# First attention of a fused two-block layer: the imaginary S5 input products of tiles 8 to 15 read a copy of the branch input whose partition halves are exchanged, in other row groups of TensorE

## The reference, cut to what matters

```python
    uf = u.astype(f32).reshape(B, S, S5_GROUPS, S5_GROUP_CH)
    ...
    bu_r = jnp.einsum('bsgh,gph->bsgp', uf, bbar_r)
    bu_i = jnp.einsum('bsgh,gph->bsgp', uf, bbar_i)
    ...
    _, _, xr, xi = lax.associative_scan(_complex_affine_combine, (a_r, a_i, bu_r, bu_i), axis=1)
    y = (jnp.einsum('bsgp,ghp->bsgh', xr, c_re.astype(f32))
         - jnp.einsum('bsgp,ghp->bsgh', xi, c_im.astype(f32)))
```

## Time and profile before

| | value |
|---|---|
| runs | 1992.41, 1983.17, 1986.96 us |
| median | 1986.96 us |
| span of the profiled execution | 1982.0 us |
| PE busy | 1873.8 us (95%) |
| DVE, ACT, POOL busy | 959.8, 523.0, 332.9 us |
| mean granted clock of PE | 0.987 |
| bytes moved | 396.88 MB |

### The profile page before, as it was taken

One profiled execution on the slowest core, in us unless ns is written; L12 is line 12 of the kernel. 1 busy time (PEld: TensorE's weight loads), 2 busy tenths in 40 slices (PEclk: granted clock), 3 DMA queues, 4 the chain that ended last, 5 costly groups with the idle time before them and its releaser, 6 DMA issues. The chain is left out here.

```text
span 1982.0 us, 27981 instructions
## 1 busy us (share of the span) xinstructions
PE 1873.8 (95%) x10606; PEld 1040.9 (53%) x10606; DVE 959.8 (48%) x2029; ACT 523.0 (26%) x1154; POOL 332.9 (17%) x297
## 2 busy tenths in 40 slices
PE   8999999999998999999999998999988999999997
PEld 3434448845443344444444443457745588888443
DVE  4987748732375232332332335623375554444643
ACT  2448831101311233333333332220255100000000
POOL 0655530000027110010010014300023000000000
PEclk9999999999999999999999999999999999999999
DMA  6129972204355999999999999613310122222311
GB/s 249 64 80 231 230 217 99 81 5 152 145 195 170 359 406 405 403 402 404 407 407 405 400 402 372 239 68 118 128 43 1 43 105 87 85 85 85 129 62 43
DMA packets 85535, 396.88 MB, mean 200 GB/s; under 512 B 13394, under 2 KB 13650, under 8 KB 60240
## 3 DMA queue, kind: packets, MB, share of 16 engines
q1 hardware_dynamic: 55728, 303.59, 40.1%
q10 hardware_dynamic: 16880, 58.52, 10.2%
q0 software_dynamic: 12848, 33.74, 4.7%
HBM read 374.66 MB, written 55.09 MB: 217 GB/s over the span
## 5 line engine op out<-in xcount | busy, mean ns | idle before, releaser
L2823 DVE COPY slab<-bank 32x512 f32<-32x512 f32 x124 | 80.8, 688 | 400.2 <-PE bank L1476 400.2
L1089 PE MATMUL bank<-ring,slab 128*128 128x512 f32 (+1 forms) x608 | 254.6, 578 | 6.5 <-DVE slab L2291 3.8
L1468 PE MATMUL bank<-slab 128*32 128x512 f32 x1536 | 228.9, 599 | 17.1 <-DMA ring<-w_exp_down 6.6
L1468 PE MATMUL bank<-ring,slab 128*32 128x512 f32 x1536 | 228.5, 598 | 14.6 <-DVE slab L2779 5.1
L1476 PE MATMUL bank<-ring,slab 128*32 128x512 f32 x512 | 228.5, 599 | 0.0
L1476 PE MATMUL bank<-slab 128*32 128x512 f32 x480 | 214.0, 599 | 0.0
L1089 PEld LDWEIGHTS bank<-ring,slab 128*128 128x128 f32 x608 | 115.7, 192 | 139.1 <-issue 130.4
L3225 POOL TENSOR_TENSOR small<-small 128x1 f32<-128x1 f32 (+2 forms) x30 | 27.5, 920 | 817.1 <-DVE small L2288 817.1
L1468 PEld LDWEIGHTS bank<-slab 128*32 128x32 f32 x1536 | 73.5, 110 | 145.7 <-issue 139.8
L1089 PE MATMUL bank<-slab,ring 128*128 128x512 f32 (+1 forms) x368 | 148.2, 559 | 1.7 <-ACT slab L1831 0.9
L1468 PEld LDWEIGHTS bank<-ring,slab 128*32 128x32 f32 x1536 | 72.3, 110 | 144.9 <-issue 142.2
(11 more groups left out here) (363 smaller groups left out, 3053.7 us busy)
## 6 DMA issues: line engine op xcount, KB each, us to landing
ring<-stream SPq DMA_DIRECT2D x173, 512.0 KB, 4.4
slab<-w_exp_gu SPq DMA_DIRECT2D x64, 1024.0 KB, 13.8
ring<-w_exp_gu SPq DMA_DIRECT2D x64, 1024.0 KB, 13.6
ring<-w_exp_down SPq DMA_DIRECT2D x32, 1024.0 KB, 22.3
slab<-w_exp_down SPq DMA_DIRECT2D x32, 1024.0 KB, 23.0
y_rows<-zeros ACTq DMA_DIRECT2D x1, 24960.0 KB, 132.0
y_rows<-slab ACTq DMA_DIRECT2D x64, 384.0 KB, 8.2
gb<-rows ACTq DMA_DIRECT2D x5, 512.0 KB, 4.4
```

Source lines behind the costliest of these rows:

```text
L1089: mm = nc.tensor.matmul(dst, lhs[k], rhs[k], start=(k == 0), stop=(k == len(lhs) - 1))
L1468: mm = nc.tensor.matmul(g_bank[32 * g:32 * g + 32, :], x[:, k, 32 * g:32 * g + 32], w[:, 512 * k:512 * k + 512], start=(k == 0), stop=(k = ...
L2823: i = nc.vector.tensor_copy(ye[b % 2][32:64, 512 * half:512 * half + 512], bank[5 + half][96:128, :])
```

## The change

The diff does five things. On the host, the imaginary input weights of tiles 8 to 15 are laid 64 partitions away from their place (modulo 128). In the ACT program, at the end of the exponentials of heads 0 and 1, two transfers from SBUF to SBUF each copy one 128 x 512 block of `uT` (blocks 2 and 3) with its lower and upper 64 partitions exchanged, into blocks 0 and 1 of slab3, where the keys of heads 0 and 1 lay; ahead of them is a wait for the fourth score tile of that head. `s5_in(i)` for `i` of 8 and above reads the copy for its imaginary product, at partitions `(r0 + 64) % 128`; at tiles 8 and 12 PE waits for the copy (`u_moved`, 32 = both halves). The imaginary states of tiles 8 and 11 move from slab3 block 0 to `s5tmp`, and that of tile 14 to slab3 block 2. POOL's wait for scores moves from tile 8 (`s` 3) to tile 14 (`s` 11).

```diff
--- before.py
+++ after.py
@@ -38,6 +38,7 @@
 XH, XD = 4, 128
 NG, NS, NCH = 32, 64, 16
 NST = NG * NS // P
+S5_TURNED = NST // 2
 NE, TOPK, NGRP, TOPG = 64, 8, 8, 4
 CAP = 96
 NOV = T * TOPK // CAP
@@ -533,7 +534,8 @@
             for g in range(2):
                 grp = 2 * i + g
                 r = 32 * (i % 4) + 16 * g
-                bm[n, r:r + 16, i // 4, 64 * g:64 * g + 64] = w[b][0, grp].T
+                rb = (r + 64) % P if n == 1 and i >= S5_TURNED else r
+                bm[n, rb:rb + 16, i // 4, 64 * g:64 * g + 64] = w[b][0, grp].T
                 cm[n, 64 * g:64 * g + 64, i, 16 * g:16 * g + 16] = w[c][0, grp].T
     return np.concatenate([bm[0].reshape(P, 512), bm[1].reshape(P, 512),
                            cm[0].reshape(P, 512), cm[1].reshape(P, 512)], 1)
@@ -614,7 +616,10 @@
         s5xr, s5xt = [unit(13), unit(14)], unit(17)
 
         def s5xi(i):
-            return unit(15 + i % 3) if i % 3 < 2 else s5tmp if i < 8 else fm(slab3, 0)
+            return unit(15 + i % 3) if i % 3 < 2 else s5tmp if i < 14 else fm(slab3, 2)
+
+        def u_turned(j):
+            return fm(slab3, j - 2)
 
         cmask = rope_q
         b_re = gb[:, 0:512].rearrange("p (j n) -> p j n", j=4)
@@ -879,6 +884,7 @@
         s5_tab, s5_z, s5_x, s5_used, s5_c = sem("s5_tab"), sem("s5_z"), sem("s5_x"), sem("s5_used"), sem("s5_c")
         rope_arg, rope_tab, krope_ready, khat_ready = sem("rope_arg"), sem("rope_tab"), sem("krope_ready"), sem("khat_ready")
         max_ready, probs_ready = sem("max_ready"), sem("probs_ready")
+        u_moved = [sem("u_moved0"), sem("u_moved1")]
         y_ready, gelu_ready = sem("y_ready"), sem("gelu_ready")
         merged_ready = sem("merged_ready")
         x2_stored, tab_zero = sem("x2_stored"), sem("tab_zero")
@@ -1103,9 +1109,17 @@
                 return [p[:, (at + k) * P:(at + k + 1) * P] for k in range(kn)]
 
             def s5_in(i):
-                r = slice(32 * (i % 4), 32 * (i % 4) + 32)
-                for name, m in (("s5r", b_re), ("s5i", b_im)):
-                    product(name, i, [m[r, i // 4, :]], [fm(uT, i // 4)[r, :]])
+                j, r0 = i // 4, 32 * (i % 4)
+                r = slice(r0, r0 + 32)
+                product("s5r", i, [b_re[r, j, :]], [fm(uT, j)[r, :]])
+                if i < S5_TURNED:
+                    product("s5i", i, [b_im[r, j, :]], [fm(uT, j)[r, :]])
+                else:
+                    if i % 4 == 0:
+                        pe.wait_ge(u_moved[j - 2], 32)
+                    r1 = (r0 + 64) % P
+                    ri = slice(r1, r1 + 32)
+                    product("s5i", i, [b_im[ri, j, :]], [u_turned(j)[ri, :]])
 
             def s5_out(i):
                 if i % 4 == 0:
@@ -1927,6 +1941,10 @@
                         x = probs(h, qt)
                         nc.scalar.activation(x, x, ACT.Exp, scale=-1.0, bias=nmax[:, qt:qt + 1],
                                              accum_out=rsum[:, qt:qt + 1]).then_inc(probs_ready, 1)
+                if h < 2:
+                    full("s", 4 * h + 3)
+                    for r in (0, 64):
+                        act.dma_start(u_turned(2 + h)[64 - r:128 - r, :], fm(uT, 2 + h)[r:r + 64, :]).then_inc(u_moved[h], 16)
                 if h >= 3 and h % 2 == 1:
                     o = (h - 3) // 2
                     copy("o", o, fm(oT, o), tile("o", o)[:, :])
@@ -3247,8 +3265,8 @@
                     pool.wait_ge(s5_x, i)
                 if i >= 2:
                     pool.wait_ge(s5_used, i - 1)
-                if i == 8:
-                    pool.wait_ge(psum_full, plan.full("s", 3))
+                if i == 14:
+                    pool.wait_ge(psum_full, plan.full("s", 11))
                 c, s = s5cos[i % 2], s5sin[i % 2]
                 zr, zi, xr, xi = s5zr[i % 2], s5zi[i % 2], s5xr[i % 2], s5xi(i)
                 op = nc.gpsimd.tensor_tensor
```

## The result

The changed kernel takes 2098.88 us (median of 4 runs, 2094.37 to 2103.09) against 1988.12 us before (4 runs). The ratio is 1.056, with a 95% interval of 1.0536 to 1.0585. The profiled execution of the changed kernel has a span of 2092.4 us and took 2094.37; before, the span was 1982.0. The difference of the spans is 110.4 us, that of the medians 110.8.

A forecast was written before the change was run, and what follows sets the result against it. PE was taken to bound the kernel, busy 1873.8 of 1982.0 us. Wait 114.3 + clock 2.9 - row groups 3.4 = +113.8 us, giving 2100.8 on the median 1986.96; predicted 2100, range 2082 to 2112.

The forecast's parts named there:

- the wait for the fill: The forecast case: at tile 8 PE waits 114.3 us for copies behind the fill, and pairs overlap; chance 0.72.
- The copy's place in the queue: On ACT's queue q10, taken to go in order, the copies land behind the fill of 24960 KB.
- When the fill lands: Fill takes 128 us, landing at 266.7; copy there at 268.0, so PE waits 114.3 us (98.5 to 118).
- The clock: After PE's wait the clock is granted at 0.50 for a while, costing 2.9 us (0 to 6).
- The other row groups: The two `s5_in` products of a tile overlap in different row groups, saving 0.86 us a pair (0 to 0.96).
- Which pairs count: Only tiles 9 to 12 of eight pairs save time, 3.4 us (0 to 6.7); from head 6 others set the pace.
- The rest: ACT's two issues, 0.45 us each, lie in its idle 3.55 us; POOL's wait, new state places and host weights cost nothing.
- rival B: ACT itself is held at the first copy's issue, freed shortly before the fill ends; at worst some 5 us added; chance 0.12.
- Two of the signs that I had named: In the profile after: second pair of copies landing at some 90 to 110 us; DVE, ACT and POOL empty from about 160.
- A: The copy passes the fill and lands in time; PE waits 0 to 3 us at tile 8, 1980 to 1987; chance 0.08.
- C: The halves of PE's array don't work at once; the 3.4 us saving is missing, 2104; chance 0.08.

The follow-up runs named there:

- run 1: Changed kernel with the fill of zeros issued by ACT behind the second pair of copies instead of ahead of the loop; 1983.95 us, ratio 0.9972.
- run 4: Changed kernel with the copies issued by SP on the weight panels' queue, the fill where it was; 1983.62 us, ratio 0.9974.
- run 5: Changed kernel, fill and copies on ACT as they are, but PE reads the original branch input in old row groups without waiting for copies; 2082.25 us, ratio 1.0458.
- Run 8: run 1 repeated (0.9980), with only tiles 8 to 12 in the other row group (0.9980), and with tiles 4 to 6 there too (0.9970).
- run 3: Kernel before the change with only the fill moved to head 1; 1989.50 us, ratio 1.0005.
- run 7: Changed kernel with a fifth of the fill ahead of the copies, four fifths behind the second pair; 2004.42 us, ratio 1.0067.
- run 2: Against run 1: copies made without the exchange, imaginary products of tiles 8 to 15 in the real ones' row group; 1993.35 us, ratio 1.0008 of before.

## Why the prediction was right, by its steps

I had forecast 2100 (2082 to 2112), slower, with the chance on the wait for the fill. The time was 2098.88. That it is within 1.1 us is partly luck: the sum was +113.8 us and the medians moved by 110.8, 3.0 less, but the median of before rose from 1986.96 to 1988.12 with a fourth run, and 0.8 us had been rounded off.

- **The copy's place in the queue.** Right, and shown by runs 1 and 4: the same copies take 2.3 us ahead of the fill, 9.8 on another queue during it, and 120.8 behind it. The order seen in the earlier trace rows, a 12 KB load that lands 13.0 us after its issue, pointed that way. It could not by itself tell order in a queue from mere traffic; run 4 does. (It was not the last to land either, as the prediction has it: a 32 KB load issued behind it, at 287.25, landed after 13.4 us, at 300.7.)
- **When the fill lands.** I took 128 us (the sum goes by 128.2); it ran in 125.7, and in 130.0 in run 5. PE's wait was 111.3 us and not 114.3, inside 98.5 to 118. The fill's own time explains 2.5 us of the difference; its earlier issue in this execution goes with an earlier tile 8 and nearly cancels.
- **The clock.** 2.9 us predicted from one gap of 4.8 us; measured 1.04 (imaginary product 2.00 instead of 0.96) + 2.53 (gate product) = 3.6. The length of the wait matters little: after waits of 13.6, 50.8 and 111.3 us the imaginary product takes 2.07 us each time and the gate product 9.32, 9.49 and 9.66.
- **The other row groups.** A pair takes 1.06 us instead of 1.91: 0.85 saved, 0.86 predicted from products of 64 rows. By the Trainium skill, "TensorE: Matmul & The Clock Gate", Part 3, as cited in the prediction, the pair would take 0.96, an estimate; the measurement decides, and stays 0.1 above.
- **Which pairs count.** Four were to count, 3.4 us; the trace gives 3.34. It adds up from the other end too: tiles 9 to 15 are seven pairs, 7 x 0.85 = 5.95, and PE's waits at the end of the attention grow by 0.8 (5.6 for 4.8), 0.9 (1.20 for 0.30) and 0.9 (a wait for ACT's gate copy that was not there before), 2.6 together. Run 8 shows it directly. With tile 8's pair whole, as in run 1, five count: 4.25 by this rule, 4.0 seen.
- **The rest.** Here I was wrong in a part that did not show in the sum. I wrote that the two issues on ACT, 0.45 us each, lie in its idle time. The first took 94.19 us. It was rival B (chance 0.12) that described this, and in place B was right: ACT was held, and freed 26 us before the fill ended. But B and the forecast do not exclude each other; B's price of up to 5 us on top was near 0, since ACT was back at work 26 us before PE was. Two of the signs that I had named failed with it: the second pair of copies, which I had put at about 160, was issued at 246.14 and landed after 18.2 us, not 90 to 110; and ACT, empty before that, was at work again from 237.87. Neither cost time, since tile 12 needs the second pair much later. Run 5 shows what B alone costs: 91 us. My reason against it, that the fill's own issue took only 0.64 us, says nothing of the one behind it.

Rivals A and C are out: no copy passed the fill on its queue, and the pairs do overlap.

**The better version.** The row groups are worth having once the copies do not stand behind the fill: 0.9972 (0.9954 to 0.9990) with the fill behind them, 0.9974 (0.9957 to 0.9991) with the copies on SP's queue, both against before. The repeat of the first gave 0.9980 (0.9960 to 1.0000). That is 3 to 6 us by the medians and 3.7 to 4.0 by the stretch from tile 8 to head 9, held against run 3, 0.2 to 0.3% of the time; the interval of the repeat reaches 1.

## What to carry to other kernels

Before a small transfer is put on a queue, look for the largest one that is still under way there, and count the bytes ahead, not the bytes of the transfer: here a copy of 128 KB took 121 us because 25.6 MB stood in front. A DMA issue is not free for its engine either: behind a large transfer the issue itself may hold the engine and all that it does for others, even when nobody waits for the data. A large transfer that nobody waits for belongs behind every small one that somebody does, or on a queue of its own; and a saving on the busiest engine counts only in stretches in which that engine does not wait for the others.

## What the runs showed of the hardware that was not expected

**An issue that holds its engine.** ACT's next issue behind the fill of 4 KB pieces was let go when some 26 to 28 us of the fill were left: 262.9 - 236.7 = 26.2 us in the changed kernel, (139.66 + 65.2) - 177.4 = 27.4 with half of the fill, (138.0 + 130.0) - 240.2 = 27.8 in run 5, where the fill was issued at 138.0 and the issue held from 143.34 to 240.2. At the fill's rate (25.56 MB in 125.7 us, 12.78 in 65.2, 25.56 in 130.0) this is 5.3 to 5.5 MB each time, about 1300 pieces of 4 KB. With 5.1 MB ahead (run 7) no issue was held. So it looks like room for a fixed amount and not for a fixed share (79% of the fill's time had passed at the release in the full case, 58% in the half case). That the limit lies in the queue is inferred from these four runs. Whether it counts pieces or bytes was not tried.

**The fill gains little from an empty machine.** Alone it moved at 204 GB/s (window 160 to 200), and it took 125.7 us in the changed kernel, where panels were loaded in its first 20 us or so only; with the panels beside it all along, it took 132.0 to 136.5 us (run 2). That is not all that the 16 DMA engines can move: later, in loads of expert weights, the page of the changed kernel shows 400 GB/s.
